# One order of the gather slots for all lists but the last, and the first four experts ahead of the next list and queries

## The reference, cut to what matters

```python
q = (xc @ w_q).reshape(C, PEER_HEADS, 2, PEER_HALF)
s = jnp.einsum('chpd,hpnd->chpn', q, subkeys)
sv, si = lax.top_k(s, 16)                      # for both halves
cand = sv[:, :, 0, :, None] + sv[:, :, 1, None, :]
best, pos = lax.top_k(cand.reshape(C, 8, 256), 16)
ids = ...                                      # 16 expert numbers per row and head
g = jax.nn.softmax(best, axis=-1)
ue = jnp.take(u, ids, axis=0); ve = jnp.take(v, ids, axis=0)
a = jax.nn.gelu(jnp.einsum('cd,chkd->chk', xc, ue), approximate=False)
return jnp.einsum('chk,chkd->cd', g * a, ve)
```

## Time and profile before

| what | value |
|---|---|
| median of three runs | 1504.35 us |
| lowest and highest run | 1503.44 and 1505.59 us |
| the profiled execution | 1506.46 us, span of the core 1504.3 us |
| busy share of the span | PE 89%, DVE 71%, ACT 40%, POOL 18% |
| gathers | 256, in all 268.45 MB |
| DMA from about 330 to 900 us | 422 GB/s |
| mean granted TensorE clock | 0.948 of full |

### The profile page before, as it was taken

One profiled execution on the slowest core, in us unless ns is written; L12 is line 12 of the kernel. 1 busy time (PEld: TensorE's weight loads), 2 busy tenths in 40 slices (PEclk: granted clock), 3 DMA queues, 4 the chain that ended last, 5 costly groups with the idle time before them and its releaser, 6 DMA issues.

```text
span 1504.3 us, 18539 instructions
## 1 busy us (share of the span) xinstructions
PE 1338.0 (89%) x6164; PEld 918.8 (61%) x6164; DVE 1073.6 (71%) x2251; ACT 598.5 (40%) x1222; POOL 276.2 (18%) x263
## 2 busy tenths in 40 slices
PE   7998899988697979789797798989999999899998
PEld 2786664434243435344343346679999876799987
DVE  4598846666767676676767757877887477788864
ACT  5343741322222221212222214565665455656652
POOL 0000002263334444444444420000000000000000
PEclk9999999999898989989898899999999999999999
DMA  9623436799999999999999996433554444244540
GB/s 396 248 112 150 187 135 283 301 423 421 421 422 422 422 422 422 422 422 422 422 421 422 421 420 234 156 145 119 190 201 170 150 142 159 112 169 176 201 156 28
DMA packets 49844, 416.18 MB, mean 277 GB/s; under 512 B 5488, under 2 KB 5616, under 8 KB 7024
## 3 DMA queue, kind: packets, MB, share of 16 engines
q0 software_dynamic: 36864, 268.45, 43.0%
q1 hardware_dynamic: 12912, 146.82, 25.7%
HBM read 414.20 MB, written 1.05 MB: 276 GB/s over the span
## 4 chain that ended last, share of the span: by engine, by line
PE 55%; DMA 17%; DVE 13%; issue 8%; POOL 4%; ACT 2%; POOLq 0%; DVEq 0%; ACTq 0%; SPq 0%
DMA arena<-in_uv,ids 15%; PE ps L1081 9%; PE ps L1333 6%; PE ps L1332 6%; PE ps L1334 6%; PE ps L1146 4%; PE ps L1148 4%; PE ps L1147 4%; POOL arena L733 2%; PE ps L936 2%; DMA ring<-in_b1w 2%; POOL ring L733 2%; DVE ring L2036 2%; PE ps L866 2%; PE ps L867 2%
## 5 line engine op out<-in xcount | busy, mean ns | idle before, releaser
L1081 PE MATMUL ps<-ring,arena 128*128 128x512 f32 x512 | 257.2, 666 | 94.0 <-ACT arena L1544 94.0
L1081 PEld LDWEIGHTS ps<-ring,arena 128*128 128x128 f32 x512 | 108.3, 215 | 238.3 <-issue 132.4
L2036 DVE CUSTOM_DVE_ANT_0 arena<-arena 128x1024 f32<-128x1024 f32 x128 | 156.6, 1226 | 123.7 <-DMA arena<-in_uv,ids 123.7
L1081 PE MATMUL ps<-arena 128*128 128x512 f32 x512 | 225.2, 597 | 4.3 <-ACT arena L1544 4.3
L564 DVE TENSOR_TENSOR arena_r<-ring,arena_r 128x1024 fp32r<-128x1024 f32 x152 | 185.0, 1223 | 58.0 <-ACT arena_r L549 57.5
L1332 PE MATMUL ps<-hH,arena_r 128*128 128x256 f32 x704 | 199.4, 283 | 0.0
L1333 PE MATMUL ps<-arena_r 128*128 128x256 f32 x704 | 199.2, 283 | 0.0
L1334 PE MATMUL ps<-hH,arena_r 128*128 128x256 f32 x704 | 199.2, 283 | 0.0
L733 POOL DMA_INDIRECT ring<-in_uv,ids x128 | 144.5, 1129 | 285.7 <-PE ps L1081 238.5
L733 POOL DMA_INDIRECT arena<-in_uv,ids x128 | 131.1, 1024 | 315.2 <-issue 256.1
L549 ACT ACTIVATE arena_r<-ring 128x1024 fp32r<-128x1024 f32 x152 | 158.9, 1053 | 58.9 <-PE ps L1148 58.6
(11 more groups left out here) (315 smaller groups left out, 1989.5 us busy)
## 6 DMA issues: line engine op xcount, KB each, us to landing
ring<-in_lw SPq DMA_DIRECT2D x39, 2048.0 KB, 7.7
ring<-in_b1w SPq DMA_DIRECT2D x18, 2048.0 KB, 8.8
wqb<-in_wq SPq DMA_DIRECT2D x8, 1024.0 KB, 9.1
ring<-in_lw SPq DMA_DIRECT2D x8, 1024.0 KB, 5.0
ring<-in_lw SPq DMA_DIRECT2D x2, 1088.0 KB, 11.3
arena<-in_uv,ids POOLq DMA_INDIRECT x128, 24.6
ring<-in_uv,ids POOLq DMA_INDIRECT x128, 22.3
cst<-in_const SPq DMA_DIRECT2D x1, 1487.5 KB, 19.1
```

The costliest lines, as they stand in the source:

```text
L1081: last = nc.tensor.matmul(ps[:, 4 + 2 * c + b, :], diag[:, k % 4, :], vrows[at[k]][:, b * 512:(b + 1) * 512], start=False, stop=(close and ...
L2036: V.tensor_tensor_reduce(out=urows[at], in0=urows[at], in1=hrow[:, c, :], scale=1.0, scalar=0.0, op0=ALU.mult, op1=ALU.add, accum_out=dots ...
```

## The change

FIRST_SLOTS gets a new order, and every list but the last uses it. The last list still puts expert k into slot k. On all engines, list 0's first group (dot products, weights, diagonals, experts) is put in front of other work. In detail:

- FIRST_SLOTS: slots 13, 14, 15 come before slots 6 and 7.
- POOL: list 1 waits for slots in the same order as all lists; list 15 waits for the place that its slot has in FIRST_SLOTS.
- DVE: four dot products of list 0, not two, and the weights of the first group stand in front of list 1's `topk`.
- PE: `keys` is cut into `all_queries` and `all_key_sums`. Experts 0 to 3 of list 0 come before the queries of head 1, experts 4 to 7 between these and their key sums, and the rest after the sums.
- ACT: the softmax of list 0 and the root of chunk 1's norm stand before the copy of the modulation row, with table loads written out; the first group's gelu and diagonals come before list 1's softmax, the other modulation row and the query copy.

```diff
-FIRST_SLOTS = (8, 9, 10, 11, 12, 0, 1, 2, 3, 4, 5, 6, 7, 13, 14, 15)
+FIRST_SLOTS = (8, 9, 10, 11, 12, 0, 1, 2, 3, 4, 5, 13, 14, 15, 6, 7)
...
-                for k in range(TOPK):
+                for k, at in enumerate(FIRST_SLOTS):
                     pool.wait_ge(pair_free, TOPK * n + k + 1)
-                    gather(n, c, k, k)
+                    gather(n, c, k, at)
...
-            pool.wait_ge(ids_ready, 2)
+            stage(1, 1)
+            with pool.Fori(1, PH - 1) as i:
+                stage(i * 2, 0)
+                stage(i * 2 + 1, 1)
+            stage(STAGES - 2, 0)
+            pool.wait_ge(ids_ready, STAGES)
             pool.sem_inc(pool_passed, 1)
             for k in range(TOPK):
-                pool.wait_ge(pair_free, NS + FIRST_SLOTS.index(k) + 1)
-                gather(1, 1, k, k)
-            with pool.Fori(1, PH) as i:
-                stage(i * 2, 0)
-                stage(i * 2 + 1, 1)
+                pool.wait_ge(pair_free, TOPK * (STAGES - 1) + FIRST_SLOTS.index(k) + 1)
+                gather(STAGES - 1, 1, k, k)
...
+            experts(0, 0, places=range(GROUP))
             pe.wait_ge(row_out, 4)
-            keys(1)
+            all_queries(1)
             mod_cols(MOD_A + MOD_B + 1, 3)
-            experts(0, 0, at=FIRST_SLOTS)
+            experts(0, 0, places=range(GROUP, 2 * GROUP))
+            all_key_sums(1)
+            experts(0, 0, places=range(2 * GROUP, TOPK))
...
             heads_in(4, range(4), 0, con("subg"))
+            softmax(0, 0)
+            table(ACT.Sqrt)
+            roots(1, 6)
+            table(ACT.Gelu)
             mod_row_out(MOD_A + MOD_B, 6)
-            roots(1, 6)
             norm2_in(1)
             queries_in(1, 3, q_done, q_out)
             rows_in(1, (0, 2))
-            mod_row_out(MOD_A + MOD_B + 1, 6)
...
+            experts(0, 0, groups=(0,))
+            softmax(1, 1)
+            table(ACT.Gelu)
+            mod_row_out(MOD_A + MOD_B + 1, 6)
             query_out(1)
-            softmax(0, 0)
-            softmax(1, 1)
-            experts(0, 0)
+            experts(0, 0, groups=range(1, GROUPS))
...
-            for k in range(2):
+            for k in range(GROUP):
                 dot(0, 0, k, FIRST_SLOTS[k])
+            dve.wait_ge(prob_done, 1)
+            run(V.reciprocal(pz[:, 0, 2:3], pz[:, 0, 1:2]))
+            weights(0, 0, 0, ENDS)
             topk(1, 0, 1)
             mod_bias(MOD_A + MOD_B, 7)
```

More of the change, by code:

```diff
@@ L1055, in _, with all_queries @@
             mod_rows(MOD_A + MOD_B + 1, 6)
-            def keys(h):
+            def all_queries(h):
                 pe.wait_ge(wq_in, 16 * h + 16)
@@ L1064, in keys, with all_key_sums @@
                 last.then_inc(q_done, 1)
+            def all_key_sums(h):
                 pe.wait_ge(q_out, h + 1)
@@ L1074, in keys, with experts @@
                 last.then_inc(s_done, 1)
-            def experts(n, c, close=False, at=range(TOPK)):
-                for k in range(TOPK):
+            def keys(h):
+                all_queries(h)
+                all_key_sums(h)
+            def experts(n, c, close=False, at=FIRST_SLOTS, places=range(TOPK)):
+                for k in places:
                     pe.wait_ge(diag_ready, TOPK * n + k + 1)
@@ L1106, in _ @@
             last.then_inc(gb_done, 1)
-            experts(STAGES - 1, 1, close=True)
+            experts(STAGES - 1, 1, close=True, at=range(TOPK))
             pe.wait_ge(gb_out, 1)
@@ L1508, in queries_in, with softmax @@
                                      ps[:, bank, 0:S].rearrange("p (s n) -> p s n", s=2), ACT.Copy).then_inc(out_done, 1)
+            def softmax(n, c):
+                act.wait_ge(best_ready, n + 1)
+                nc.scalar.activation(prob[:, c, :], best[:, c, :], ACT.Exp, bias=pz[:, c, 0:1],
+                                     accum_out=pz[:, c, 1:2]).then_inc(prob_done, 1)
             roots(1, 4)
@@ L1527, in query_out, with experts @@
                     .then_inc(q_out, 1)
[L1529 to L1537, removed]
+            def experts(n, c, ends=ENDS, groups=range(GROUPS)):
+                for g in groups:
+                    end, start = ends[g], ends[g - 1] if g else 0
                     act.wait_ge(dots_ready, TOPK * n + end)
@@ L1560, in _ @@
             experts(STAGES - 2, 0)
-            experts(STAGES - 1, 1, LAST_ENDS)
+            experts(STAGES - 1, 1, LAST_ENDS, range(len(LAST_ENDS)))
             table(ACT.Sqrt)
@@ L2037, in dot, with products @@
                                        op0=ALU.mult, op1=ALU.add, accum_out=dots[:, c, k:k + 1]).then_inc(dots_ready, 1)
-            def products(n, c, ends=ENDS):
+            def products(n, c, ends=ENDS, at=FIRST_SLOTS):
                 for g, end in enumerate(ends):
@@ L2043, in products @@
                     for k in range(start, end):
-                        dot(n, c, k, k)
+                        dot(n, c, k, at[k])
                         if k == start and g > 0:
@@ L2056, in _ @@
             dve.wait_ge(row_out, 2)
-            for k in range(2):
+            for k in range(GROUP):
                 dot(0, 0, k, FIRST_SLOTS[k])
+            dve.wait_ge(prob_done, 1)
+            run(V.reciprocal(pz[:, 0, 2:3], pz[:, 0, 1:2]))
+            weights(0, 0, 0, ENDS)
             topk(1, 0, 1)
             mod_bias(MOD_A + MOD_B, 7)
-            for k in range(2, TOPK):
+            for k in range(GROUP, TOPK):
                 dot(0, 0, k, FIRST_SLOTS[k])
[L2063 to L2066, removed]
+                if k % 4 == 0 and k > GROUP:
                     weights(0, 0, k // 4 - 1, ENDS)
@@ L2085, in _ @@
             V.tensor_tensor(fg2[:, :], con("fg"), con("fg"), ALU.mult).then_inc(fg2_ready, 1)
-            products(STAGES - 1, 1, LAST_ENDS)
+            products(STAGES - 1, 1, LAST_ENDS, range(TOPK))
             dve.wait_ge(gb_done, 1)
```

## The result

The changed kernel takes 1496.36 us, the median of five runs. Four of them lie between 1494.22 and 1496.79 and have a median of 1496.32; the fifth took 2694.28 us and is left out of the ratio. The kernel before, timed beside it, takes 1503.68. The ratio is 0.9938, with an interval of 0.9923 to 0.9953: faster, by 0.5 to 0.8%. The medians alone give 0.9951, which lies at the upper end of the interval. The forecast was 1494.2 us, in a range of 1490.5 to 1499.5.

The account below looks back on a forecast made before the run. The gather part was taken as bound by the DMA engines, by bytes and time not moving; 10.1 + 0.6 - 0.5 = 10.2 us off 1504.35 gave 1494.2 us, in a range of 1490.5 to 1499.5.

Parts of the forecast that it names:

- The hole: At the DMA engines around list 1's start: a big hole of 10.1 us and a small one of 0.6 us close.
- Root, queries, numbers: On ACT, PE and DVE before list 1: root at about 243.4, queries 3.9 us, list 1's numbers at about 266.0.
- Closed twice over: At the big hole: slot order alone would do most of it, slot 8's gather arriving at 283.5 in place of 292.2.
- The fifth gather: In list 1: released at 279.5, it arrives at the DMA engines at 282.0, over 10 us early.
- The thin queue: At the last list: less than one gather queued may leave some engines dry; 0.5 us given back, bounds 0 and 2.6.
- The seventh gather: In the last list: waits for list 14's fifteenth expert, at the engines 876.6 against 878.2, slack 1.6 us.
- The first rival: In the last list: the queue runs dry, giving 2 to 5 us back, 1496.5 to 1499 us; chance 0.15.
- The second: Before list 1: DVE's new wait for the gelu holds `topk` and numbers, hole closes only in part, 1500 us; chance 0.05.
- The third: At list 1 or the middle lists: slots are not the limit or time is lost again, 1504 us; chance 0.05.
- The fourth: In list 14: PE stays at 1.2 GHz for all the list, slower, some 1517 us; chance 0.04.
- the prediction's step from the rule to every place where DVE is busy: On POOL: DVE instructions hold the descriptor port, so long issues come where DVE is busy; first rival's chance 0.2 by it.
- the median of the runs lies 2.1 lower: For the whole kernel: the runs' median lies 2.1 us below the profiled execution, forecast at 1496.3, giving 1494.2 us.

Follow-up runs that it names:

- The root alone: In the kernel before, ACT does the root of chunk 1's norm before copying the modulation row; stretch 666.28 us, median 1502.53 us, ratio 0.9976.
- the order alone: Kernel before with only the new FIRST_SLOTS and its orders on POOL, DVE and PE; stretch 660.78 us, median 1497.70 us, ratio 0.9941.
- the moves alone: Changed kernel with the old slot order, keeping the moves on DVE, PE and ACT and the earlier root; stretch 660.37 us, median 1497.07 us.
- the run with 12 dot products: Changed kernel with twelve dot products of list 0, not four, before list 1's `topk`; stretch 664.66 us, median 1502.31 us, ratio 0.9975.
- the run with four experts late: Changed kernel, each last-list gather waiting for four more experts of list 14 than needed, at most the sixteenth; stretch 664.48 us, median 1501.32 us.
- the changed kernel again: Changed kernel rerun without an edit, as reference for the other runs; stretch 659.59 us, median 1496.48 us, ratio 0.9934.
- last list 2 and 4 experts late: Changed kernel, last-list gathers waiting for two or four more experts of list 14 than needed; medians 1497.09 and 1501.32 us.

## Why the prediction was right

**The hole, 10.1 and 0.6 us.** Lost against 422 GB/s between 240 and 885 us, summed over stretches of 5 us, are 11.2 us before and 1.2, 0.8 and 1.7 us in the three profiles of the changed kernel. That is 9.5 to 10.4 us, and the stretch itself is 9.9 to 10.2 us shorter. The sum said 10.2.

**Root, queries, numbers.** This profile's first gather is 0.63 us later than in the one that I worked from, so 0.6 is added to the times of the sum here. The root was foreseen at 244.0 and is done at 244.13. Chunk 1's queries took the 3.9 us that I chose for them. `topk` was foreseen at 255.5, and what stands before it ended at 255.15. The first four experts were to begin at 262.0 and began at 261.91. List 1's numbers (266.6) and the fifth expert (278.4) came at 266.3 and 277.42, the latter 1.0 us early, since the chain behind the queries took 1.5 us and not 2.3. The root alone was worth 3.5 us, where the 2.33 us of idle time and 1.6 us of faster queries make 3.9.

**Closed twice over.** It was said that the order alone "would do most of it". It did 9.0 of 10.2, and the moves alone 9.4.

**The fifth gather** of list 1 was to be at the engines at 282.6; issued at 280.22, with the 1.7 us of the earlier trace rows it is there at 281.9, and the engines had work until about 293.

**The thin queue.** I took 0.5 between bounds of 0 and 2.6, without a row that gave the value; the rows between 865 and 875 show 0.24, 0.12 and 0.45 in the three profiles. The engines did not stand still together. The seventh gather, foreseen at 878.2 less 1.6 and the 1.7 to the engines, or 874.9 in the time of the kernel before, came at 865.51, and 874.9 less 9.3 for the shift of the end is 865.6.

**The first rival** (the queue runs dry in the last list) has its conditions shown by the delays: it begins 2 us further on and then costs 3.2 us for the next 2.8 us of delay. By the sum, one POOL issue of 2.5 us at the seventh gather would just have used up its slack; that issue took 0.94 us in all three profiles of the changed kernel. **The second** (DVE's new wait) was 15 us from its threshold, as read, and the wait was 1.01 us. **The third** (no effect) falls with 9.9 us. **The fourth** (PE at half clock in list 14) occurred in its first part and not for the whole list: after 9.80 us of idle time the clock is low until about 841, which costs 2.7 us, and from 845 to 870 it is 1.00 with experts at 1.74 us. The kernel before has the same (eight experts in 16.70 us from 845.37, then eight in 13.90), so the slacks, read from its times, had this loss in them already. In the run with 12 dot products PE is idle from 275 to 280 and for more than half of the next five, and the clock is 0.50 from 280 to 290. No POOL issue waits for PE there before 295.36, so that PE's delay lay in the standstill that DVE's had made already.

**POOL's long issues.** Two issues take 1.99 and 1.98 us, against 0.94 as a rule, and DVE runs dot products beside them (268.61). They cost nothing here, since the engines had work queued. In this profile 32 of the 256 issues take 1.4 us or more, and 31 of these lie beside a dot product for over 0.5 us; of the 122 that lie beside none the longest takes 1.45 us. But 58 issues lie beside one for as long and stay under 1.4 us. So a dot product goes with nearly every long issue and does not make each one long. The Trainium skill ("SBUF — State Buffer", the box on the DVE blocks DMA trap) lays such delays to DVE instructions in a two-port mode. The trace agrees in that the long issues stand beside DVE's work, but no row shows the mode of a dot product, so the prediction's step from the rule to every place where DVE is busy is not shown. Where the queue is empty a long issue does cost: the first packet follows the end of the issue by 0.70 us in the kernel before (292.09, after 0.94 us) and by 0.72 us in the run with four experts late (858.09, after 1.57 us).

**The median is 2.2 us above the forecast** although the sum was right to 0.3 us. The step that was off is "the median of the runs lies 2.1 lower": I subtracted from a median of three runs that was low against the later ones. Whether that was chance or the chip of that series is not shown. The profiled execution was to take 1496.3 and took 1496.79; the changed kernel's medians are 1496.36, 1496.48 and 1496.77 in three series, while those of before are 1503.68, 1506.75, 1506.50 and 1505.73. So the difference between medians is 7.3 to 10.3 us, and 10 us is the difference of the stretch.

## What to carry to other kernels

Where a queue of transfers is saturated, count the bytes, and the time in which it moves fewer; look for the one place where the rate falls, and read the slack of every other place before asking what a faster engine gives. When two edits both bring the same late transfer forward, their gains need not add (9.0 and 9.4 us alone, 10.2 together here): run each alone before keeping both. A slack that is read from a trace can be measured by delaying what it covers in two steps, one inside and one beyond it.

## What the runs showed of the hardware that was not expected

**A standstill late in a row of transfers is in part paid back at its end.** The last 4 us before the last landing, in two halves; first the kernel before, whose standstill was 600 us earlier, then the changed kernel again, then the run with the last list 4 experts late, whose standstill was 45 us earlier:

```profile
901.47:903.47 2.00, 2.00 (x6) 0.85 (x5) 0.88 (x4) 0.49 (x2) 0.00 (x0) 1.00 0.71 295
903.47:905.47 2.00, 2.00 (x6) 0.86 (x5) 0.94 (x3) 0.49 (x2) 0.00 (x0) 1.00 0.09 37
```

```profile
891.00:893.00 2.00, 2.00 (x6) 0.83 (x5) 0.88 (x4) 0.49 (x2) 0.00 (x0) 1.00 0.70 291
893.00:895.00 2.00, 2.00 (x6) 0.88 (x5) 0.94 (x3) 0.49 (x2) 0.00 (x0) 1.00 0.05 20
```

```profile
895.91:897.91 2.00, 2.00 (x6) 0.85 (x5) 0.88 (x4) 0.49 (x2) 0.00 (x0) 1.00 1.01 422
897.91:899.91 2.00, 2.00 (x6) 0.86 (x5) 0.93 (x3) 0.49 (x2) 0.00 (x0) 1.00 0.36 147
```

In the four microseconds 2.4 and 2.5 us of full rate are lost in the first two, 1.3 in the third. Over all profiles it is 1.9 to 2.6 us in the ten without a late standstill, and 1.2 and 1.3 in the two with one (last list 2 and 4 experts late). That is why this run lost 6.2 us more of the full rate by 885 us than the changed kernel, and landed only 4.9 later. The reading was that the sixteen DMA engines drift apart over many gathers and begin again together after a standstill.

The traces bear out the second half. They record sixteen completion events for each gather, as many as there are DMA engines. From the first to the last of the sixteen it is 1.4 us for the gathers of 261 to 276 us in the changed kernel run again, 3.1 us between 400 and 430, 3.4 at 845 and 2.8 for the last gather. With four experts late it is 3.5 us ahead of the standstill at 855, then 0.6 to 1.2 us up to the last gather. Over all profiles the last gather has 2.3 to 3.2 us in the ten and 1.0 to 1.1 in the two. After its early standstill the run with 12 dot products has 1.3 us, but 2.6 again at the end. The first half was not quite so: the spread doesn't grow from gather to gather but holds for many and then steps up (2.3 to 3.3 us at 341 in the changed kernel run again). Around 874, behind the thin queue, it steps down from 3.3 to 2.8. What makes the steps up, and that each event is one engine's, is not shown.

**The beginning varies more than the rest.** In the ten profiles of the experiments the first gather is issued between 234.12 and 239.30 us, without an edit that would account for it, while the stretch of the same kernel repeats to 0.3 us (659.91, 659.59, 659.91). The latest of them (root alone) has a granted clock of 0.91 in its first 40 us and 0.94 from 120 to 150, where the earliest has 1.00 in both; from 150 to 180 it is 0.94 against 1.00. No run tests whether that is the cause. In the profiles of the changed kernel the spans, 1494.7, 1493.3 and 1495.4, go with the first gather at 236.31, 235.42 and 237.13. If the runs without a profile differ in the same way, that bounds what a median of three can tell of this kernel.
